# A hybrid decoder step on one core: the sample group's new retention states from row quarters of 32 tokens, two heads at once, with more zero products behind them

## What is computed

```python
s_new = s * chunk_decay + jnp.einsum('bhjd,bhje->bhde', kc * k_decay, vc)
```

## Time and profile before

| | |
|---|---|
| median of 3 runs | 813.89 us (813.34 to 815.07) |
| the profiled execution's own time | 814.6 us |
| its span, first to last instruction | 812.8 us |
| mean granted TensorE clock | 0.994 of full |
| TensorE matmul busy | 799.0 us (98%), 4078 passes |
| VectorE busy | 599.8 us (74%) |
| ScalarE busy | 476.3 us (59%) |
| GpSimd busy | 326.3 us (40%) |

### The profile page before, as it was taken

How to read it: one execution, slowest core, us unless ns; L and a number is a source line. 1 busy time by engine, 2 the same in 40 slices (tenths; PEclk the granted TensorE clock), 3 DMA queues, 4 the chain that set the end, 5 groups by cost and what they waited for, 6 DMA issues and landing times.

```text
span 812.8 us, 11902 instructions
## 1 busy us (share of the span) xinstructions
PE 799.0 (98%) x4078; PEld 638.9 (79%) x4078; DVE 599.8 (74%) x950; ACT 476.3 (59%) x808; POOL 326.3 (40%) x225
## 2 busy tenths in 40 slices
PE   9999999999999999999999999999999999999996
PEld 6887788878868888888588887888788678888861
DVE  5444646574789999999754456647757899999986
ACT  5633342622479888887663432443334798888874
POOL 0016995410042245664100199915001333665530
PEclk9999999999999999999999999999999999999998
DMA  8832223325939999998853222231387599999967
GB/s 294 290 113 66 77 78 105 105 79 191 412 137 379 369 365 384 395 371 292 275 175 118 74 79 76 55 98 71 105 325 305 202 417 367 383 381 392 335 237 290
DMA packets 57295, 188.18 MB, mean 232 GB/s; under 512 B 10862, under 2 KB 11886, under 8 KB 49036
## 3 DMA queue, kind: packets, MB, share of 16 engines
q1 hardware_dynamic: 44476, 156.57, 53.5%
q0 software_dynamic: 10368, 23.09, 7.7%
q10 hardware_dynamic: 2400, 7.87, 2.5%
HBM read 173.00 MB, written 29.39 MB: 249 GB/s over the span
## 4 chain that ended last, share of the span: by engine, by line
PE 88%; DVE 5%; DMA 3%; issue 1%; ACT 1%; SPq 0%; POOL 0%; ACTq 0%; POOLq 0%; DVEq 0%
PE ps L497 13%; PE ps L1473 12%; PE ps L1475 12%; PE ps L1474 11%; PE ps L501 10%; PE ps L500 10%; PE ps L1481 3%; PE ps L499 3%; PE ps L1672 2%; PE ps L1452 2%; DMA back<-y_d 2%; DMA hg<-xn_d,rowidx 1%; PE ps L1697 1%; PE ps L1712 1%; PE ps L1423 1%
## 5 line engine op out<-in xcount | busy, mean ns | idle before, releaser
L497 PE MATMUL ps<-wh,hT 128*128 128x512 f32 x408 | 163.5, 401 | 0.2
L910 POOL DMA_INDIRECT y_d<-y,rowidx x32 | 112.7, 3521 | 125.7 <-DVE y L2197 117.9
L2172 DVE TENSOR_TENSOR gul<-wgu,eh 128x1024 fp32r<-128x1024 f32 x128 | 150.1, 1211 | 0.3 <-ACT eh L1158 0.3
L2163 DVE SCALAR_TENSOR_TENSOR wl<-raw,gcol,wh 128x512 fp32r<-128x512 f32 x80 | 76.7, 961 | 77.2 <-ACT wh L1127 77.1
L1158 ACT ACTIVATE eh<-wgu 128x1024 fp32r<-128x1024 f32 x128 | 128.5, 1058 | 4.5 <-PE ps L1475 3.6
L501 PE MATMUL ps<-wh,lT 128*128 128x512 f32 x313 | 122.3, 391 | 0.0
L500 PE MATMUL ps<-wl,hT 128*128 128x512 f32 x313 | 121.9, 389 | 0.0
L1473 PE MATMUL ps<-eh,hgTh 128*128 128x512 f32 x240 | 96.6, 403 | 0.4 <-issue 0.4
L1475 PE MATMUL ps<-eh,hgTl 128*128 128x512 f32 x240 | 93.9, 391 | 0.0
L1474 PE MATMUL ps<-gul,hgTh 128*128 128x512 f32 x240 | 93.5, 390 | 0.0
L1127 ACT ACTIVATE wh<-raw,gcol 128x512 fp32r<-128x512 f32 x80 | 57.3, 719 | 59.6 <-PE ps L499 56.1
(11 more groups left out here) (271 smaller groups left out, 1630.6 us busy)
## 6 DMA issues: line engine op xcount, KB each, us to landing
wgu<-in_gate_up SPq DMA_DIRECT2D x64, 1024.0 KB, 12.6
wdn<-in_w_down SPq DMA_DIRECT2D x64, 512.0 KB, 12.1
raw<-in_w_in SPq DMA_DIRECT2D x79, 256.0 KB, 2.7
raw<-in_w_out SPq DMA_DIRECT2D x32, 256.0 KB, 2.8
back<-y_d SPq DMA_DIRECT2D x16, 512.0 KB, 5.9
s<-in_state_ret POOLq DMA_DIRECT2D x8, 512.0 KB, 4.2
xn_d<-xf ACTq DMA_DIRECT2D x8, 512.0 KB, 6.5
x_in<-in_x_cols SPq DMA_DIRECT2D x8, 288.0 KB, 5.2
```

The costliest lines, as they stand in the source:

```text
L497: pe.matmul(out, both, w_h, start=first, stop=False)
L910: pool.indirect_dma_start(out=y_d, out_offset=bass.IndirectOffsetOnAxis(ap=rowidx[:, 1, e:e + 1], axis=0), in_=y[s][:, :], in_offset=None, ...
L2163: ve.scalar_tensor_tensor(out=wl[S % SPL][:, :], in0=raw[S % RAW][:, :], scalar=gcol[:, 0, L, s % KC:s % KC + 1], in1=wh[S % SPL][:, :].bi ...
L2172: ve.tensor_tensor(gu_pair(gul, gul3, e, s, p), gu_pair(wgu, wgu3, e, s, p), gu_split(e, p)[:, :].bitcast(F32), ALU.subtract).then_inc(glo, 1)
```

## The change

1. **Masks.** `seqm` becomes 4 columns wide. Row p belongs to column (p // 8) % 4, on all 128 partitions.
2. **Values.** The masked values of two heads share one tile of [128, 4, 128]: head one on partitions 0 to 63, head two on 64 to 127. GpSimd makes `v_late` with two instructions of 64 x 512, one behind the other with a semaphore between them, and without the wait for `on_tr`. ScalarE makes `v_end` with four copies of 128 x 128 in place of sixteen of 64 x 128; the half behind the last expert is gone.
3. **Keys.** The late heads' keys go to the two partition halves of one [128, 128] tile; ScalarE's copies of the sample tile's keys cover 64 partitions. `kv_d` is laid out by head, so `kv_end` is one tile with two heads on the partition halves. It is written and read in pieces of 512 bytes and 1 KB where it was 1 KB and 2 KB.
4. **Products.** `new_states` issues four products, one for each (head, bank): keys and masked values of 32 partitions, 0, 32, 64 and 96, into four different banks, with one semaphore increment behind the last. In the routing stretch the four old states come first (one before the position products as before, two between these and the table products, one behind the table products), then the four quarters. The consumers wait for the one increment.
5. **Zero products.** 14 in place of 1 in front of the first expert, 16 in place of 4 between the layers, 11 in one place instead of 4 and 4 at the end.

```diff
-    seq_mask = (p[:, None] // DECS == np.arange(DECB)[None]) & (p[:, None] < NSAMP)
+    seq_mask = (p[:, None] // DECS) % 4 == np.arange(4)[None]
...
-        kv_end = tile("kv_end", [P, 2 * LATE, P], off=region + 32 * 1024)
+        kv_end = tile("kv_end", [P, 2, P], off=region + 32 * 1024)
-        kd_late = tile("kd_late", [P, NH - LATE, P], off=wpool_at)
+        kd_late = tile("kd_late", [P, P], off=wpool_at)
-        vb = [tile(f"vb{i}", [P, DECB, P], off=(d_at, d_at + 4096, gn_at, d_at + 4096)[i]) for i in range(NH)]
+        v_end = tile("v_end", [P, 4, P], off=d_at)
+        v_late = tile("v_late", [P, 4, P], off=gn_at + 2048)
-        kv_d = nc.dram_tensor("kv_d", (NSAMP, 2 * LATE, P), F32).ap()
+        kv_d = nc.dram_tensor("kv_d", (LATE, NSAMP, 2, P), F32).ap()
...
-                sp.dma_start(kv_d[:, 0:LATE, :], kd[0][0:NSAMP, 0:LATE, :]).then_inc(late_st, 16)
+                sp.dma_start(kv_d[:, :, 0, :].rearrange("h t d -> t h d"), kd[0][0:NSAMP, 0:LATE, :]).then_inc(late_st, 16)
...
-                sp.wait_ge(vb_done, NH * L + NH - LATE)
+                sp.wait_ge(vb_done, 2 * L + 1)
...
-                sp.dma_start(kv_end[0:NSAMP, :, :], kv_d).then_inc(gain_ld, 16)
+                sp.dma_start(kv_end[:, :, :], kv_d.rearrange("h t w d -> (h t) w d")).then_inc(gain_ld, 16)
...
+                pool.wait_ge(sg_done, NT * (L + 1))
+                pool.wait_ge(o_mm, NT * L + LAST)
                 for h in range(LATE, NH):
-                    if h == 3:
-                        pool.wait_ge(on_tr, NT * L + 5)
-                    pool.tensor_tensor(vb[h][:, :, :], over(zq(LAST, "v")[:, h * P:(h + 1) * P], DECB),
-                                       c("seqm").unsqueeze(2).to_broadcast([P, DECB, P]), ALU.mult).then_inc(vb_done, 1)
+                    last = pool.tensor_tensor(v_late[NSAMP * (h - LATE):NSAMP * (h - LATE) + NSAMP, :, :],
+                                              over(zq(LAST, "v")[0:NSAMP, h * P:(h + 1) * P], 4), seqm[0:NSAMP], ALU.mult)
...
-            def end_mask(L, h):
+            def end_mask(L):
                 sc.wait_ge(gain_ld, end_loads(L))
-                for b in range(DECB):
-                    last = sc.activation(vb[h][0:NSAMP, b, :], kv_end[0:NSAMP, LATE + h, :], ACT.Copy, scale=c("seqm")[0:NSAMP, b:b + 1])
+                for b in range(4):
+                    last = sc.activation(v_end[:, b, :], kv_end[:, 1, :], ACT.Copy, scale=c("seqm")[:, b:b + 1])
...
                 sc.wait_ge(dpe, 2 * NE * (L + 1))
-                end_mask(L, 1)
...
-            def late_new(L, h, n):
-                pe.wait_ge(vb_done, NH * L + h - LATE + 1)
-                pe.matmul(ps[B_LATE[h - LATE][n]][:, :], kd_late[:, h - LATE, :], vb[h][:, 4 * n:4 * n + 4, :],
-                          start=False, stop=True).then_inc(skv_mm, 1)
+            def new_states(banks, keys, values, first):
+                for h in range(2):
+                    for n in range(2):
+                        rows = slice(NSAMP * h + 32 * n, NSAMP * h + 32 * n + 32)
+                        last = pe.matmul(ps[banks[h][n]][:, :], keys[rows, :], values[rows, :, :], start=first, stop=True)
+                last.then_inc(skv_mm, 1)
...
+            def end_states(L):
                 pe.wait_ge(gain_ld, end_loads(L))
                 old = L + 1 < NL
                 if old:
+                    for h in range(LATE):
+                        for n in range(2):
+                            pe.matmul(ps[B_END[L][h][n]][:, :], ident, s0_end[h][:, 4 * n:4 * n + 4, :], start=True, stop=False)
+                pe.wait_ge(vb_done, 2 * L + 2)
+                new_states(B_END[L], kv_end[:, 0, :], v_end, not old)
...
                 last.then_inc(pos_mm, 1)
-                late_new(L, 2, 0)
+                late_old(L, *LATE_STEPS[1])
+                late_old(L, *LATE_STEPS[2])
...
                 last.then_inc(tab_mm, 1)
-                for h, n in LATE_STEPS[1:]:
-                    late_old(L, h, n)
-                    late_new(L, h, n)
-                idle_turns(3, 1)
+                late_old(L, *LATE_STEPS[3])
+                pe.wait_ge(vb_done, 2 * L + 1)
+                new_states(B_LATE, kd_late, v_late, False)
+                idle_turns(3, 14)
...
                 if L + 1 < NL:
-                    end_state(L, 0)
-                    end_state(L, 1)
-                    idle_turns(0, 4)
-            end_state(NL - 1, 0)
+                    end_states(L)
+                    idle_turns(0, 16)
+            end_states(NL - 1)
             own_rows(3)
-            end_state(NL - 1, 1)
             own_rows(LAST)
+            pe.wait_ge(s_new, LATE * (NL - 1) + 1)
+            idle_turns(B_END[NL - 1][0][0], 11)
             pe.wait_ge(gdiag_done, 4)
```

More of the change, by code:

```diff
@@ L950, in _ @@
                     gate_gain(L, t)
+                pool.wait_ge(sg_done, NT * (L + 1))
+                pool.wait_ge(o_mm, NT * L + LAST)
+                seqm = c("seqm").unsqueeze(2).to_broadcast([P, 4, P])
                 for h in range(LATE, NH):
-                    if h == 2:
-                        pool.wait_ge(sg_done, NT * (L + 1))
-                        pool.wait_ge(o_mm, NT * L + LAST)
-                    if h == 3:
-                        pool.wait_ge(on_tr, NT * L + 5)
-                    pool.tensor_tensor(vb[h][:, :, :], over(zq(LAST, "v")[:, h * P:(h + 1) * P], DECB),
-                                       c("seqm").unsqueeze(2).to_broadcast([P, DECB, P]), ALU.mult).then_inc(vb_done, 1)
+                    last = pool.tensor_tensor(v_late[NSAMP * (h - LATE):NSAMP * (h - LATE) + NSAMP, :, :],
+                                              over(zq(LAST, "v")[0:NSAMP, h * P:(h + 1) * P], 4), seqm[0:NSAMP], ALU.mult)
+                    if h < NH - 1:
+                        link(last)
+                last.then_inc(vb_done, 1)
+                pool.wait_ge(vb_done, 2 * L + 1)
                 pool.wait_ge(gain_ld, 64 * L + 16)
@@ L1083, in late_state @@
             def late_state(L, h, n):
[L1085 removed]
+                sc.wait_ge(skv_mm, 2 * L + 1)
                 sc.activation(s_out[h - LATE][:, 4 * n:4 * n + 4, :], ps[B_LATE[h - LATE][n]][:, :].rearrange("p (b e) -> p b e", b=4),
@@ L1113, in end_state @@
             def end_state(L, h):
-                sc.wait_ge(skv_mm, 6 * L + 4 + h + 1)
+                sc.wait_ge(skv_mm, 2 * L + 2)
                 for n in range(2):
@@ L1221, in expert @@
                     y_evac(L, e - 1, (s + 2) % 3, n[0])
-                    end_mask(L, 0)
+                    end_mask(L)
             def pool_u(L, g):
@@ L1256, in key_decay @@
                     sc.wait_ge(kv_mm, LAST * L + t - 1)
+                n = tokens(t)
                 for h in range(NH):
-                    dst = kd_late[:, h - LATE, :] if t == LAST and h >= LATE else kd[t % 2][:, h, :]
-                    last = sc.activation(dst, zq(t, "k")[:, h * P:(h + 1) * P], ACT.Copy,
-                                         scale=c("kdec", 1 + NL)[:, 1 + L if t == LAST else 0, h:h + 1])
+                    late = t == LAST and h >= LATE
+                    dst = kd_late[NSAMP * (h - LATE):NSAMP * (h - LATE) + NSAMP, :] if late else kd[t % 2][0:n, h, :]
+                    last = sc.activation(dst, zq(t, "k")[0:n, h * P:(h + 1) * P], ACT.Copy,
+                                         scale=c("kdec", 1 + NL)[0:n, 1 + L if t == LAST else 0, h:h + 1])
                 last.then_inc(kd_done, 1)
@@ L1760, in end_state @@
                 if old:
-                    for n in range(2):
-                        pe.matmul(ps[B_END[L][h][n]][:, :], ident, s0_end[h][:, 4 * n:4 * n + 4, :], start=True, stop=False)
-                pe.wait_ge(vb_done, NH * L + NH - LATE + h + 1)
-                for n in range(2):
-                    last = pe.matmul(ps[B_END[L][h][n]][:, :], kv_end[0:NSAMP, h, :], vb[h][0:NSAMP, 4 * n:4 * n + 4, :], start=not old, stop=True)
-                last.then_inc(skv_mm, 1)
+                    for h in range(LATE):
[3 more added lines that the diff above has]
+                new_states(B_END[L], kv_end[:, 0, :], v_end, not old)
             def own_rows(t):
@@ L2346, in sample_state @@
             def sample_state(L, h):
-                ve.wait_ge(skv_mm, 6 * L + 4 + h + 1)
+                ve.wait_ge(skv_mm, 2 * L + 2)
                 for n in range(2):
```

3 lines of the change are left out of this document (1 added, 2 removed).

## The result

The kernel after takes 818.92 us (median of four runs, 816.57 to 819.74) where the kernel before took 813.71 beside it: a ratio of 1.005, 95% interval 1.0035 to 1.0065. Forecast was 814.1, with a range to 817.2. The medians lie 5.2 us apart; the ratio is a comparison of all the runs and not the quotient of the medians, and 0.5% of this kernel is 4 us. I go by the ratio: the change costs about 4 us, where the forecast was no change to speak of. The profiled execution of after took 816.57 us with a span of 814.8; it is the fastest of the four, so its trace shows only part of the loss (2.0 us of span over before).

The account below looks back on a forecast made before the run. TensorE holds 88% of the chain, but landings or VectorE close its waits in all three places; 0 + 0.28 - 0.1 + 0 = +0.2 on the profiled 814.6 gives 814.8, median 814.1, range 812.6 to 817.2.

Parts of the forecast that it names:

- passes in order: Rival: row quarters start in strict order, each second pass holding up the next quarter; 3.0 us more, 817.0; chance 0.10.
- one after the other: Rival: the four row quarters run serially, 3.48 us instead of 0.87; 7.8 us more, 821.8; chance 0.05.
- X: Time of the four row quarters together in TensorE: taken as 0.87 us, bounds 0.87 to 3.48.
- the column quarters: Sample attention's products, 32 quarter passes in the 1.06 us of 8 whole ones; the basis for pricing row quarters at 0.87.
- The routing stretch of layer 0: Old states, quarters and zero products there all end before the waits they fill; cost 0.
- between the layers: TensorE done at 398.3 instead of 398.8, but transposes wait for VectorE's sum: 0.1 us gained; ScalarE's saved masking worth 0.
- the end: TensorE's work 9.2 us against 10.4, hidden inside the 6.80 us load of returned rows that the chain goes through; cost 0.
- Routing, layer 1: Two old states at low clock start the table products 0.28 us later, paid in full; 0 where the clock stays high.
- a low granted clock behind a wait that TensorE did not have: Last of the listed signs that would show the forecast wrong; no place or size given.
- something slower that I don't see (..., a landing): Unseen slower outcome, such as a consumer of the single increment or a landing; no size given; chance 0.04.
- The clock rival: Rival: layer 1's low clock stretch does not come again, saving about 0.5 us, 813.3; chance 0.12.

Follow-up runs that it names:

- before_dead: The kernel before with only dead code added: 13 and 44 zero products in the never taken branches of layers 0 and 1; 816.96 us, ratio 1.002.
- the repeat: The kernel after, unaltered, measured again in the session of the experiments; 818.81 us, ratio 1.0038 (1.0025 to 1.0051).
- tail_busy: The kernel after with 14 zero products instead of 4 ahead of the wait for tile 3's last row; 818.63 us, ratio 1.0039.
- the kernel without the eleven: The kernel after without the eleven zero products added at the end, other filling kept; 816.93 us, ratio 1.0018.
- the two float32 variants: The float32 filling with only dead code added in never taken branches, (10, 18) or (0, 47) products for the two layers; 815.31 and 815.69 us, ratios 1.0005 and 1.0014.
- pad_before: The kernel before with 26 instructions of already met waits at TensorE's start and 25 dead products in layer 0's never taken branch; 818.05 us, ratio 1.0033.
- the float32 filling: The kernel after with 14, 16, 11 and 4 zero products made as 3, 4, 3 and 1 float32 products; 814.68 us, ratio 1.0003.

## Why the prediction was wrong

**Right.** The row quarters run side by side, in order and without ScalarE waiting: the rivals *passes in order* and *one after the other* are out. X was 0.87, or 0.97 with the one change of rows; measured is 1.08 from start to start. The Trainium skill's 3.07 (TensorE: Matmul & The Clock Gate, Part 3, measured speedup), by which I had estimated 1.13, came closer than the column quarters did; it changed nothing, since all of it is covered. The routing stretch of layer 0 cost 0 as said. That what is saved in TensorE between the layers and at the end frees it only for more waiting was right too: after is ahead there by 2.8 us (395.08 against 397.91) and by 3.1 (794.25 against 797.39) and gains nothing.

**A size off.** Routing, layer 1: +0.28 was priced with the low clock of before. The low stretch did not come in after's profile, and the tables were 0.08 late. The first expert of layer 1 then lost 0.2 us more, where the prediction had nothing added.

**The step that failed** is *between the layers* and *the end*, "Worth 0" and "Cost 0; both ends of what moves lie inside the 6.80 us". I took the load of the returned rows as fixed and priced the zero products by their time in TensorE alone, 0.22 each, hidden. Each is also two instructions, and 49 of them move every later code fetch. So the loads that close both waits were not fixed. At the end an issue in front of them grew by 0.6 to 0.85 us and a load by up to 1.3 (that of tile 3's row from 5.5 to 6.8 in after, the fourth from 6.80 to 8.03 in `before_dead`). Between the layers the first row's load grew by 0.8 to 1.9 (3.56 to between 4.34 and 5.46). Of after's 4 us, dead code takes back some 2.1 at the end (1.0012 against 1.0038 in the repeat; 3.1 against 1.005), and the one fetch left between the layers shows as 1.0 us in the line-up of that run. The prediction's own last sign of being wrong, "a low granted clock behind a wait that TensorE did not have", did come, at 803 us. Chance "something slower that I don't see (..., a landing)": 0.04. It should have been the rival for the other side, since the page of before lists the 29 instruction packets, and the change adds code ahead of two places where a landing is the path.

**The reading of the diff** that was wrong (4 and 4 removed) hid one thing: the four zero products behind the second group stand behind the late row, and with the low clock took 1.91 us. As `tail_busy` shows, this too cost nothing to measure.

**The clock rival** was right as far as it went: the low stretch of layer 1 was absent from after's profile, and from 625 to 631 us after made up 0.6 us on before, near the 0.5 priced. But such a stretch comes and goes from one execution to the next, and what it gives is small beside the end. What the rival did not have is the low clock that the filling prevents, 2.7 and 2.5 us in the first expert of the two layers.

## What to carry to other kernels

An instruction can have a price beside its time: code comes by DMA in blocks of 256 instructions, and a block that was fetched while short loads on the path were issued and landing went with 1 to 2 us here. Where a change adds filling, or code of any kind, look at where the instruction packets lie, before and after, against the loads that end the waits. Try filling waits with few long instructions (a float32 product of 512 columns lasts 0.9 us and is four instructions, where bf16 needs eight or nine; here this took the ratio from 1.0038 to 1.0003), and test a suspicion of this kind with dead code in a branch that is never taken: it moves the fetches and leaves every executed instruction as it is. Then look in the trace where the fetches went, since several tries here missed. The row quarters themselves bring nothing here, as both places end with a DMA chain (last expert's rows out, issue, rows back).

## What was not expected of the hardware

- A 16 KB code packet (0.9 to 1.7 us long) and SyncE's issue of another DMA beside it: 1.0 to 1.3 us instead of 0.43. How the two hinder each other is not shown, only that they come together and that moving the one by dead code moves the other. In the kernel without the eleven a packet of 1.74 us went with a third issue that started 2.2 us behind the end of the second, where before has 0.5.
- A packet is not always harmful where it should be, nor a late landing always explained: with no packet among the loads at the end the slowest row took 6.9 to 7.7 us in eight of ten profiles, but 7.9 and 8.2 in two. That stays open.
- When a fetch starts could not be told from an instruction's place in the code alone: the two float32 variants were placed by it and missed.
- In all kernels with the change the scatter of the last expert's rows took 3.50 to 3.7 us on the chain of the end, in the three without it (before, `pad_before`, `before_dead`) 3.19. That is 0.3 to 0.5 us of the end which no experiment took apart.
- Against it, in eight of the eleven kernels with the change the first of the early rows of layer 1 (the other half of the experts' results, loaded from 776 us on) landed so soon that VectorE stood 0.34 us or less for it, where it stood 1.00 in before, and TensorE caught up by some 0.7 us before 784. In the repeat and in the kernel with the end kept busy VectorE stood 0.94 and 1.04 and little was caught up. What decides this was not tested. It helps to leave the float32 filling where before is; a version that beats before was not found.
